# Sparse and forgetting attention on one core: row spreads of inverse roots and forget biases by DMA, index products in four groups

## The chip, the core and the metric

The kernel runs on one core of a Trainium2 chip. The metric is the device time of one execution in microseconds (us); less is better. It computes in float32 throughout. Large matrix products are made from three passes: an operand is rounded to a short form ("hi", type fp32r) with the rest kept as a second one ("lo"), and hi*hi, hi*lo and lo*hi are summed in PSUM.

## What is computed

A trunk of two layers on 512 positions of width 1024. Each layer has a SwiGLU feed-forward half step, a mixer, another half step and a normalisation. The mixer of layer one is DSA, that of layer two FoX. Cut to what matters here:

```python
# DSA: an index score picks 128 keys per query
dots  = relu(einsum('bqhd,bsd->bqhs', iq, ik))        # 8 index heads of 64
score = einsum('bqh,bqhs->bqs', iw, dots)             # masked, then top_k
k = rms_norm(k, k_gain)                               # 2 key heads of 128
# FoX: 8 heads of 128
k = rms_norm(k, k_gain)
cum = cumsum(log_sigmoid(fz + f_bias), axis=1)        # one row per head
logits = q @ k.T * scale + cum_of_query - cum_of_key  # the query's term drops out of softmax
p = softmax(where(causal, logits, -inf))
```

## The kernel before

Activations lie transposed: 128 features on the partitions, 512 positions along a row. Weights come in **units** of 1024 x 128. SP loads a unit (512 KB) into a ring of four, ACT rounds it (`hi`, line 411), DVE or POOL makes the rest (`lo`, lines 751 and 345), and PE runs 24 matmuls of 512 columns with it (lines 1297, 1298, 1302; `section` and `unit`). There is no planner: each engine's program is written out by hand and the order of its lines is the order of the work. Semaphores tie the engines together.

**DSA, index part.** Four units give the eight index heads, two heads per unit: an even head on partitions 0 to 63, an odd one on 64 to 127. A product (`score`, lines 1493 to 1495) is three matmuls over 64 rows and 256, 384 or 512 columns, for one head and one of three query blocks (the first block needs none). `dots(g)` makes six, waiting for the copies in PSUM that ACT has still to take. ACT applies relu (line 574), DVE sums with the weights `iw` (lines 1086, 1089). The order is head by head: three blocks of one head, then three of the next. PE runs `dots(0)`, `dots(1)`, unit 4, `dots(2)`, `dots(3)`, then units 5 to 7. Then DVE runs `top_k` for three blocks: 16 rounds each of a maximum and a replacement, with the k work between them. PE meanwhile makes the eight q units.

**Normalising k.** k has positions along the row, so its inverse root has to lie along the row too, the same on all 128 partitions. PE sums the squares with a column of ones (lines 1574 and 1762), DVE turns that to a variance (`var`, lines 1134 and 1260), and POOL raises it to -1/2 (`job`, line 315). The root is then one number per partition and block. DVE splits it in hi and lo (`split_roots`, lines 778 and 779) and PE spreads it with eight matmuls against the identity (`spread`, line 1361). DVE multiplies k by the bank (lines 1141 and 1268), ACT rounds k, and DVE or POOL makes its lo part.

**FoX, head j.** PE runs unit q, unit k, the bias (`fox_bias`, lines 1741 and 1742), ten transposes of the head before (`fox_turn`, line 1708), half of unit v, the values of the head before (`fox_pv`, line 1720), the sums of squares (line 1762), the other half of v, half of the gate unit, the spread, four transposes of v (line 1772), the rest of the gate unit, and the scores (`fox_score`, lines 1493 to 1495 and 1731). The bias is row j of `cum` on all partitions: two matmuls over eight rows of `cum_hi` and `cum_lo`, copied by ACT to `fox_nb` (`keep_nb`, line 684) and added by DVE at line 1278. `forget_sums` (lines 1206 to 1211) makes `cum` once, in head 0, before the k multiplication of line 1268.

```python
                pe.wait_ge(root_ready, 8 + j)
                spread(bank[FOX_RB[1]], 9 + j, NB).then_inc(k_rb, 1)
                pe.wait_ge(evicted, n + 3)
```

Of the kernel before, what the change touches and what calls it, by code (L numbers as in the profile page):

```python
# [90 lines left out]
def build(nc, xt, cvec, columns, mod_t, w_units, out):  # L91
    ctx = ExitStack()
    with ctx:
# [92 lines left out]
        cum_hi, cum_lo = hid_hi[0:HEADS, KT - 1, :], hid_lo[0:HEADS, KT - 1, :]  # L186
# [7 lines left out]
        K_BANK, V_BANK = (2, 6), (6, 1)  # L194
# [37 lines left out]
        qk_sq, qk_stat, k_rb, k_ready = sem("qk_sq"), sem("qk_stat"), sem("k_rb"), sem("k_ready")  # L232
# [161 lines left out]
        ROOTS_BEFORE = [0, 1, 3, 4, 5, 6, 15, 16]  # L394
# [8 lines left out]
        def _(act):  # L403
# [278 lines left out]
            def keep_nb(j):  # L682
                act.wait_ge(nb_done, j + 1)
                act.activation(fox_nb[:, j % 2, :], bank[OB], ACT.Copy).then_inc(nb_ready, 1)

            for j in range(HEADS):
# [35 lines left out]
                if j == 0:  # L722
                    keep_nb(0)
# [13 lines left out]
        def _(dve):  # L737
# [341 lines left out]
            def index_sums(g):  # L1079
                for m in range(6 * g, 6 * g + 6):  # L1080
                    b, head = m % 3 + 1, m // 3
# [3 lines left out]
                    if head == 0:  # L1085
# [148 lines left out]
            for j in range(HEADS):  # L1234
# [21 lines left out]
                lo(n + 5)  # L1256
# [611 lines left out]
```

## Time and profile before

| | |
|---|---|
| median of 3 runs | 2023.62 us (2021.04 to 2023.71) |
| the profiled execution | 2023.55 us, its span 2021.7 us |
| busy PE / PE weight load | 98% / 81% |
| busy DVE / ACT / POOL | 55% / 36% / 10% |
| granted TensorE clock, mean | 0.993 |
| DMA | 253.97 MB, mean 126 GB/s |

The span is what the profile covers; the 1.85 us between it and the execution's own time lie around it. An end of a matmul is modelled: a 512-column matmul reads 0.39 us, but the next begins 0.23 us after it. So times on PE are read as distances between starts.

### The profile page before, as it was taken

What the parts mean: (1) busy time and instruction counts of PE and PEld (TensorE: products, weight loads), DVE (VectorE), ACT (ScalarE), POOL (GpSimd) and SP (SyncE); (2) the same over time, 40 slices, a digit from 0 to 9 for tenths busy, and PEclk for the clock granted to TensorE, in tenths of its full rate; (3) what the DMA queues carried; (4) which work ended last, traced back from release to release, by engine and by line L of the source; (5) the groups of instructions that cost most, each with busy time, mean ns of one, the idle gap of its engine ahead of it and who ended that gap; (6) DMA issues with size and microseconds to landing.
All of it is one profiled execution on the core that took longest, in us unless ns stands there. A gap on an engine that the chain in (4) does not pass through costs nothing.

```text
span 2021.7 us, 23587 instructions
## 1 busy us (share of the span) xinstructions
PE 1986.2 (98%) x9174; PEld 1645.4 (81%) x9174; DVE 1109.7 (55%) x1705; ACT 726.7 (36%) x1066; POOL 193.4 (10%) x221
## 2 busy tenths in 40 slices
PE   6999999999999999999999999999999999999997
PEld 4888888888888888888888888877888888888886
DVE  7665553788757655636863553475454573333334
ACT  5222312554644222225322222345555442222223
POOL 3110000026600100000110100000000000000000
PEclk9999999999999999999999999999999999999998
DMA  8665542322025655623553632222221122323221
GB/s 318 239 214 180 184 156 88 100 87 74 22 98 194 216 172 194 189 77 108 188 190 104 205 125 83 94 84 64 73 72 54 63 94 104 104 83 108 81 87 57
DMA packets 72014, 253.97 MB, mean 126 GB/s; under 512 B 8025, under 2 KB 8153, under 8 KB 71938
## 3 DMA queue, kind: packets, MB, share of 16 engines
q1 hardware_dynamic: 53280, 185.62, 28.0%
q0 software_dynamic: 18512, 67.26, 10.0%
q8 instruction: 46, 0.75, 0.1%
q14 instruction: 30, 0.25, 0.0%
q10 hardware_dynamic: 146, 0.09, 0.0%
HBM read 250.70 MB, written 2.10 MB: 125 GB/s over the span
## 4 chain that ended last, share of the span: by engine, by line
PE 76%; issue 19%; DVE 3%; POOL 1%; ACT 1%; DMA 0%; POOLq 0%; SPq 0%; DVEq 0%; ACTq 0%
PE bank L1297 23%; PE bank L1302 23%; PE bank L1298 23%; PE bank L1762 1%; PE bank L1720 1%; PE bank L1361 1%; PE bank L1651 1%; PE bank L1493 1%; PE bank L1495 1%; DVE dve_tmp L876 1%; PE bank L1494 0%; PE bank L1708 0%; DVE wlo L751 0%; PE bank L1626 0%; DVE h_lo L869 0%
## 5 line engine op out<-in xcount | busy, mean ns | idle before, releaser
L1297 PE MATMUL bank<-h_hi,whi 128*128 128x512 f32 x1808 | 712.3, 394 | 6.8 <-DVE wlo L751 4.5
L1298 PE MATMUL bank<-h_hi,wlo 128*128 128x512 f32 x1808 | 706.1, 391 | 0.0
L1302 PE MATMUL bank<-h_lo,whi 128*128 128x512 f32 x1808 | 594.1, 390 | 0.5 <-POOL h_lo L331 0.5
L411 ACT ACTIVATE whi<-wraw 128x1024 fp32r<-128x1024 f32 x338 | 347.1, 1053 | 267.0 <-PE bank L1302 263.9
L751 DVE TENSOR_TENSOR wlo<-wraw,whi 128x1024 fp32r<-128x1024 f32 x324 | 389.2, 1223 | 57.3 <-ACT whi L411 56.5
L1297 PEld LDWEIGHTS bank<-h_hi,whi 128*128 128x128 f32 x1808 | 341.2, 189 | 79.3 <-issue 5.0
L1302 PEld LDWEIGHTS bank<-h_lo,whi 128*128 128x128 f32 x1808 | 340.5, 188 | 73.1 <-POOL h_lo L331 1.2
L1298 PEld LDWEIGHTS bank<-h_hi,wlo 128*128 128x128 f32 x1808 | 341.0, 189 | 68.6
L1297 PE MATMUL bank<-hid_hi,whi 128*128 128x512 f32 x832 | 324.3, 390 | 0.0
L1302 PE MATMUL bank<-hid_lo,whi 128*128 128x512 f32 x832 | 323.7, 389 | 0.0
L1298 PE MATMUL bank<-hid_hi,wlo 128*128 128x512 f32 x832 | 323.7, 389 | 0.0
L956 DVE TENSOR_TENSOR dve_tmp<-act_tmp,bank 128x512 f32<-128x512 f32 x85 | 58.5, 689 | 458.6 <-ACT act_tmp L478 458.6
L478 ACT ACTIVATE act_tmp<-bank 128x512 f32<-128x512 f32 x85 | 51.0, 600 | 624.3 <-PE bank L1302 624.2
L1302 PEld LDWEIGHTS bank<-hid_lo,whi 128*128 128x128 f32 x832 | 156.2, 188 | 32.6
L1298 PEld LDWEIGHTS bank<-hid_hi,wlo 128*128 128x128 f32 x832 | 156.2, 188 | 32.4
L1297 PEld LDWEIGHTS bank<-hid_hi,whi 128*128 128x128 f32 x832 | 156.2, 188 | 32.0
L904 DVE SCALAR_TENSOR_TENSOR xT<-bank,gate,xT 128x512 f32<-128x512 f32 x96 | 72.1, 751 | 170.0 <-PE bank L1302 169.9
L315 POOL TENSOR_TENSOR rstd<-var,minus_half 128x8 f32<-128x8 f32 (+2 forms) x19 | 33.3, 1753 | 1119.0 <-DVE var L786 759.6
L763 DVE CUSTOM_DVE_ANT_0 arena<-arena,cond,cols 128x1024 f32<-128x1024 f32 x96 | 121.1, 1280 | 0.0
L310 POOL DMA_DIRECT2D arena<-in_mod_t_dram x96 | 50.7, 529 | 309.0 <-DVE modc L763 309.0
L962 DVE TENSOR_TENSOR hid_lo<-dve_tmp,hid_hi 128x512 fp32r<-128x512 f32 x88 | 60.5, 687 | 21.3 <-ACT hid_hi L481 19.2
L428 ACT ACTIVATE sq<-xT 128x512 f32<-128x512 f32 x42 | 26.6, 633 | 72.2 <-DVE xT L904 72.2
(239 smaller groups left out, 1390.1 us busy)
## 6 DMA issues: line engine op xcount, KB each, us to landing
wraw<-in_w_units_dram SPq DMA_DIRECT2D x306, 512.0 KB, 3.5
arena<-in_mod_t_dram POOLq DMA_DIRECT2D x96, 512.0 KB, 4.9
mod_tile<-in_mod_t_dram POOLq DMA_DIRECT2D x32, 512.0 KB, 4.7
wraw<-in_w_units_dram SPq DMA_DIRECT2D x32, 384.0 KB, 3.4
arena<-in_mod_t_dram SPq DMA_DIRECT2D x12, 512.0 KB, 7.9
xT<-in_xt_dram SPq DMA_DIRECT2D x8, 256.0 KB, 4.5
out_dram<-xT SPq DMA_DIRECT2D x8, 256.0 KB, 2.3
mod_tile<-in_mod_t_dram SPq DMA_DIRECT2D x2, 512.0 KB, 9.5
```

What stands on the lines that cost most here:

```text
L310: pool.dma_start(tile_slot(t), mod_t[t, :, :]).then_inc(ring_in[t % MOD_RING], 16)
L315: pool.tensor_tensor(rstd[:, j % 2, at:at + n], var[:, j % 2, at:at + n], minus_half[:, 0:n], ALU.pow)\
L411: act.activation(whi[:, s % RING, :, :], wraw[:, s % RING, :, :], ACT.Copy).then_inc(hi_ready, 1)
L478: act.activation(act_tmp[:, q, :], bank[s % 4][:, :], ACT.Silu).then_inc(act_out, 1)
L751: dve.tensor_tensor(wlo[:, s % RING, :, :], wraw[:, s % RING, :, :], whi[:, s % RING, :, :].bitcast(F32), ALU.subtract).then_inc(lo_ready, 1)
L763: dve.tensor_tensor_reduce(out=src, in0=src, in1=cond_wide if t < MOD_FIRST else cond[:, :], scale=1.0, scalar=cols[:, col:col + 1], op0=A ...
L904: dve.scalar_tensor_tensor(out=xT[:, bass.ds(i * 4 + d, 1), :], in0=bank[at].unsqueeze(1), scalar=g[:, bass.ds(i * 4 + d, 1)], in1=xT[:, b ...
L956: dve.tensor_tensor(dve_tmp[:, q, :], act_tmp[:, q, :], bank[(s + 1) % 4][:, :], ALU.mult)\
L962: dve.tensor_tensor(hid_lo[:, n, :], dve_tmp[:, q, :], hid_hi[:, n, :].bitcast(F32), ALU.subtract).then_inc(hid_ready, 1)
L1297: pe.matmul(dst, whi[:, w, k, :], hi_, start=first, stop=False)
L1298: pe.matmul(dst, wlo[:, w, k, :], hi_, start=False, stop=False)
L1302: return pe.matmul(dst, whi[:, s % RING, k, :], lo_, start=False, stop=last)
```

## The change

1. **k roots by DMA.** POOL writes the root to a row in device memory (`k_roots`), waits, and reads it back on all 128 partitions: in DSA once for both key heads, in FoX once per head. `split_roots` and `spread` go for k. DVE multiplies by the copy in SBUF, reading it with a step of four elements (`from_row`).
2. **Forget biases by DMA.** `cum` is written to device memory once; `fetch_bias(j)` reads row j on all partitions into `fox_nb`. `fox_bias`, `keep_nb` and the split of `cum` go.
3. **FoX order.** For j > 0 the sums of squares come right after `fox_turn`, in bank 5, and DVE takes `var` before the next `lo` and the output of the head before.
4. **Index products.** `dot_at` makes even and odd heads take turns, product by product. The four groups lie one after `dots(0)`, in the middle and at the end of unit 4, and in the middle of unit 5.

```diff
+def dot_at(m):
+    return m % 3 + 1, 2 * (m // 6) + m % 2
...
+        fox_kb, dsa_kb = sq[:, 1, :], pt_lo[:, 0:KV_HEADS * SEQ].bitcast(F32)
...
@@ POOL, DSA
             job(2, 8)
+            pool.wait_ge(rstd_ready, 3)
+            pool.dma_start(k_roots[HEADS:HEADS + KV_HEADS, :].rearrange("g (p b) -> p g b", b=NB),
+                           rstd[:, 0, 0:KV_HEADS * NB].rearrange("p (g b) -> p g b", g=KV_HEADS)).then_inc(root_out, 16)
+            pool.wait_ge(root_out, 16)
+            pool.dma_start(dsa_kb.rearrange("p (g n) -> p g n", g=KV_HEADS),
+                           k_roots[HEADS:HEADS + KV_HEADS, :].unsqueeze(0).broadcast_to([P, KV_HEADS, SEQ]))\
+                .then_inc(root_in, 16)
...
@@ POOL, FoX
+            def fetch_bias(j):
+                if j > 1:
+                    pool.wait_ge(masked, NB * (HEADS + j - 1))
+                pool.dma_start(fox_nb[:, j % 2, :], cum_rows[j:j + 1, :].broadcast_to([P, SEQ])).then_inc(nb_in[j % 2], 16)
+
             for j in range(HEADS):
                 job(9 + j, 8)
+                pool.wait_ge(rstd_ready, 10 + j)
+                pool.dma_start(k_roots[j, :].rearrange("(p b) -> p b", b=NB), rstd[:, (9 + j) % 2, NB:2 * NB])\
+                    .then_inc(root_out, 16)
+                pool.wait_ge(root_out, 16 * (j + 2))
+                if j:
+                    pool.wait_ge(qk_normed, 2 + j)
+                pool.dma_start(fox_kb, k_roots[j:j + 1, :].broadcast_to([P, SEQ])).then_inc(root_in, 16)
+                if j == 0:
+                    pool.wait_ge(cum_ready, 1)
+                    pool.dma_start(cum_rows[:, :], cum[0:HEADS, :]).then_inc(cum_out, 16)
+                    pool.wait_ge(cum_out, 16)
+                    fetch_bias(0)
+                if j + 1 < HEADS:
+                    fetch_bias(j + 1)
...
@@ ACT, FoX
                 if j:
-                    keep_nb(j)
                     fox_rounds(j - 1)
...
@@ DVE, DSA
             top_k(1, 13, 16)
-            split_roots(2, 2 * NB)
             top_k(2, 0, 4)
+            dve.wait_ge(root_in, 16)
             for g in range(KV_HEADS):
-                dve.wait_ge(k_rb, g + 1)
-                dve.tensor_tensor(dsa_k[:, g, :], dsa_k[:, g, :], bank[K_BANK[g]][:, :], ALU.mult)\
+                dve.tensor_tensor(by_block(dsa_k[:, g, :]), by_block(dsa_k[:, g, :]),
+                                  from_row(dsa_kb[:, g * SEQ:(g + 1) * SEQ]), ALU.mult)\
                     .then_inc(qk_normed, 1)
...
@@ DVE, forget_sums and FoX
-                link(dve.tensor_tensor_scan(cum[0:HEADS, :], sq[0:HEADS, 0, :], z, 0.0, ALU.mult, ALU.subtract))
-                link(dve.tensor_copy(cum_hi, cum[0:HEADS, :]))
-                dve.tensor_tensor(cum_lo, cum[0:HEADS, :], cum_hi.bitcast(F32), ALU.subtract).then_inc(cum_ready, 1)
+                dve.tensor_tensor_scan(cum[0:HEADS, :], sq[0:HEADS, 0, :], z, 0.0, ALU.mult, ALU.subtract)\
+                    .then_inc(cum_ready, 1)
...
                     fox_splits(j - 1)
-                lo(n + 5)
+                else:
+                    lo(n + 5)
+                dve.wait_ge(qk_stat, 10 + j)
+                dve.tensor_scalar(var[:, (9 + j) % 2, 0:8], bank[FOX_STAT][:, 0:8], 1.0, HD * EPS, ALU.mult, ALU.add)\
+                    .then_inc(var_ready, 1)
                 if j:
+                    lo(n + 5)
                     fox_output(j - 1)
-                dve.wait_ge(qk_stat, 10 + j)
-                dve.tensor_scalar(var[:, (9 + j) % 2, 0:8], bank[STAT][:, 0:8], 1.0, HD * EPS, ALU.mult, ALU.add)\
-                    .then_inc(var_ready, 1)
-                split_roots(9 + j, 2 * NB)
                 lo(n + 6)
                 if j == 0:
                     forget_sums()
-                dve.wait_ge(k_rb, 3 + j)
+                dve.wait_ge(root_in, 16 * (j + 2))
                 dve.wait_ge(evicted, n + 2)
-                dve.tensor_tensor(fox_qk[:, 1, :], fox_qk[:, 1, :], bank[FOX_RB[1]], ALU.mult).then_inc(qk_normed, 1)
+                dve.tensor_tensor(by_block(fox_qk[:, 1, :]), by_block(fox_qk[:, 1, :]), from_row(fox_kb), ALU.mult)\
+                    .then_inc(qk_normed, 1)
                 dve.wait_ge(qk_rounded, 4 + 2 * j)
                 dve.tensor_tensor(qk[:, 3, :], fox_qk[:, 1, :], qk[:, 1, :].bitcast(F32), ALU.subtract)\
                     .then_inc(k_ready, 1)
                 split_v(j % 2, bank[FOX_VB], 3 + j)
-                dve.wait_ge(nb_ready, j + 1)
...
@@ PE, DSA
                 for m in range(6 * g, 6 * g + 6):
-                    b, head = m % 3 + 1, m // 3
+                    b, head = dot_at(m)
...
             dots(0)
-            dots(1)
-            plain(4)
-            dots(2)
-            dots(3)
-            for n in range(5, 8):
+            for n in range(4, 6):
+                begin(U + n, U + n - 1)
+                for part in range(2):
+                    section(U + n, bank[(U + n) % 2], 4 * part, 4 * part + 4, h_hi, h_lo)
+                    if n == 4 or part == 0:
+                        dots(2 * n - 7 + part)
+            for n in range(6, 8):
                 plain(n)
...
                 if j:
                     dsa_q_stat(j - 1)
-                if j == 0:
-                    pe.wait_ge(root_ready, 3)
-                    for g in range(KV_HEADS):
-                        spread(bank[K_BANK[g]], 2, NB * g).then_inc(k_rb, 1)
...
@@ PE, FoX
-            def fox_bias(j):
-                if j == 0:
-                    pe.wait_ge(cum_ready, 1)
-                else:
-                    pe.wait_ge(nb_ready, j)
-                if j > 1:
-                    pe.wait_ge(gated, j - 1)
-                head = ident_r[0:HEADS, j:j + 1].broadcast_to([HEADS, P])
-                pe.matmul(bank[OB], head, cum_hi, start=True, stop=False)
-                pe.matmul(bank[OB], head, cum_lo, start=False, stop=True).then_inc(nb_done, 1)
+            def fox_stat(j):
+                pe.wait_ge(qk_sq, 12 + 2 * j)
+                for q in range(2):
+                    for b in range(NB):
+                        ins = pe.matmul(bank[FOX_STAT][:, NB * q + b:NB * q + b + 1], act_tmp[:, q, b * P:(b + 1) * P],
+                                        ones[:, 0:1], start=True, stop=True)
+                ins.then_inc(qk_stat, 1)
...
                 if j:
-                    fox_bias(j)
                     fox_turn(j - 1)
+                    fox_stat(j)
                 begin(n + 2, n + 1 if j else U)
                 section(n + 2, bank[n % 2], 0, 4, h_hi, h_lo)
                 if j:
                     fox_pv(j - 1)
-                pe.wait_ge(qk_sq, 12 + 2 * j)
-                for q in range(2):
-                    for b in range(NB):
-                        ins = pe.matmul(bank[STAT][:, NB * q + b:NB * q + b + 1], act_tmp[:, q, b * P:(b + 1) * P],
-                                        ones[:, 0:1], start=True, stop=True)
-                ins.then_inc(qk_stat, 1)
+                else:
+                    fox_stat(j)
                 section(n + 2, bank[n % 2], 4, KT, h_hi, h_lo)
                 begin(n + 3, n + 2)
                 section(n + 3, bank[(n + 1) % 2], 0, 4, h_hi, h_lo)
-                pe.wait_ge(root_ready, 8 + j)
-                spread(bank[FOX_RB[1]], 9 + j, NB).then_inc(k_rb, 1)
                 pe.wait_ge(evicted, n + 3)
                 for b in range(NB):
                     ins = pe.transpose(bank[FOX_VB][:, b * P:(b + 1) * P], fox_vT[:, b * P:(b + 1) * P], ident[:, :])
                 ins.then_inc(v_turned, 1)
                 section(n + 3, bank[(n + 1) % 2], 4, KT, h_hi, h_lo)
-                if j == 0:
-                    fox_bias(0)
                 fox_score(j)
```

**PE, FoX, head 1, from the end of unit k.** Line 1708 (after: 1745) is `fox_turn`, 1762 (after: 1773) the sums of squares. Before:

```order
L1302 MATMUL bank<-h_lo,whi 128x512
L1741 MATMUL bank<-hid_hi,ident_r 128x512 [waits nb_ready]
L1742 MATMUL bank<-hid_lo,ident_r 128x512
L1708 MATMUL bank<-ident,arena 128x128 [waits fox_split,v_ready,p_ready]
L1708 MATMUL bank<-ident,arena 128x128 x9
L1297 MATMUL bank<-h_hi,whi 128x512 [waits evicted,lo_ready]
```

After:

```order
L1341 MATMUL bank<-h_lo,whi 128x512
L1745 MATMUL bank<-ident,arena 128x128 [waits fox_split,v_ready,p_ready]
L1745 MATMUL bank<-ident,arena 128x128 x9
L1773 MATMUL bank<-ones,act_tmp 128x1 [waits qk_sq]
L1773 MATMUL bank<-ones,act_tmp 128x1 x7
L1336 MATMUL bank<-h_hi,whi 128x512 [waits evicted,lo_ready]
```

The two bias matmuls are gone and the sums of squares have come up to here from behind `fox_pv`.

**POOL, FoX, heads 0 and 1.** Before, POOL had one operation per head here. After:

```order
L334 TENSOR_TENSOR rstd<-var,minus_half 128x8 [waits var_ready]
L415 DMA k_roots<-rstd 128x4 [waits rstd_ready]
L420 DMA sq<-k_roots 128x512 [waits root_out]
L423 DMA cum_rows<-arena 8x512 [waits cum_ready]
L410 DMA arena<-cum_rows 128x512 [waits cum_out]
L410 DMA arena<-cum_rows 128x512
L334 TENSOR_TENSOR rstd<-var,minus_half 128x8 [waits var_ready]
L415 DMA k_roots<-rstd 128x4 [waits rstd_ready]
L420 DMA sq<-k_roots 128x512 [waits qk_normed,root_out]
L410 DMA arena<-cum_rows 128x512 [waits masked]
```

Each head now has a chain of two transfers behind its root, and the bias of the next head follows it on the same queue.

**PE, DSA, the end of `dots(0)`.** Before, `dots(1)` follows at once:

```order
L1493 MATMUL bank<-hid_hi 128x512
L1494 MATMUL bank<-hid_lo,hid_hi 128x512
L1495 MATMUL bank<-hid_hi,hid_lo 128x512
L1493 MATMUL bank<-hid_hi 128x256 [waits relu_ready,evicted]
L1494 MATMUL bank<-hid_lo,hid_hi 128x256
```

After, the first half of unit 4 stands between them:

```order
L1532 MATMUL bank<-hid_hi 128x512
L1533 MATMUL bank<-hid_lo,hid_hi 128x512
L1534 MATMUL bank<-hid_hi,hid_lo 128x512
L1336 MATMUL bank<-h_hi,whi 128x512 [waits evicted,lo_ready]
L1337 MATMUL bank<-h_hi,wlo 128x512
```

## Rows read from the trace of the kernel before

**Rows 1.** Waits of PE, whole span: us in total, times, longest.

```profile
PE bank L1762 <- ACT act_tmp L700: 2.8, 1, 2.8
```

**Rows 2.** Timeline of PE, FoX head 2: start us, duration us, instruction.

```profile
1414.81 0.39 PE L1298 MATMUL bank<-h_hi,wlo 128*128 128x512 f32 x1
1415.04 0.39 PE L1302 MATMUL bank<-h_lo,whi 128*128 128x512 f32 x1
...
1416.01 1.31 PE L1708 MATMUL bank<-ident,arena 128*128 128x128 f32 x10
...
1421.77 1.89 PE L1762 MATMUL bank<-ones,act_tmp 128*128 128x1 f32 x16
...
1429.08 1.00 PE L1361 MATMUL bank<-ident_r,root 128*128 128x128 f32 x8
1429.92 0.63 PE L1772 MATMUL bank<-ident,arena 128*128 128x128 f32 x4
...
1433.13 0.22 PE L1493 MATMUL bank<-qk 128*128 128x128 f32 x1
```

**Rows 3.** Timelines of DVE and POOL, FoX head 2.

```profile
1423.97 0.16 DVE L1260 TENSOR_SCALAR var<-bank 128x8 f32<-128x8 f32 x1
...
1424.21 1.64 POOL L315 TENSOR_TENSOR rstd<-var,minus_half 128x8 f32<-128x8 f32 x1 [29.50 <-DVE var L1260]
...
1428.14 1.23 DVE L751 TENSOR_TENSOR wlo<-wraw,whi 128x1024 fp32r<-128x1024 f32 x1 [1.88 <-ACT whi L411]
1430.12 0.69 DVE L1268 TENSOR_TENSOR arena<-arena,bank 128x512 f32<-128x512 f32 x1 [0.76 <-PE bank L1361]
```

**Rows 4.** DMA issues: count, KB each, median us from issue to landing.

```profile
arena<-in_mod_t_dram POOLq DMA_DIRECT2D x96, 512.0 KB, 4.9
...
mod_tile<-in_mod_t_dram SPq DMA_DIRECT2D x2, 512.0 KB, 9.5
...
act_tmp<-arena POOLq DMA_DIRECT2D x1, 16.0 KB, 2.0
```

**Rows 5.** Timelines of DVE and PE, FoX head 0.

```profile
1366.02 0.41 DVE L1210 CAST hid_hi<-arena 8x512 fp32r<-8x512 f32 x1
...
1367.08 0.67 DVE L1268 TENSOR_TENSOR arena<-arena,bank 128x512 f32<-128x512 f32 x1
...
1369.19 0.33 PE L1493 MATMUL bank<-qk 128*128 128x128 f32 x1 [1.13 <-DVE qk L1270]
```

**Rows 6.** Busy us (count) of PE, weight load, DVE, ACT, POOL; clock; DMA.

```profile
1360.00:1395.00 35.00, 33.87 (x169) 27.46 (x169) 18.98 (x37) 17.65 (x31) 1.64 (x1) 0.95 0.20 61
```

**Rows 7.** Timeline of PE, DSA index products and what follows them.

```profile
415.39 0.38 PE L1493 MATMUL bank<-hid_hi 64*128 64x256 f32 x1 [0.58 <-DVE hid_lo L1100]
...
416.43 0.28 PE L1494 MATMUL bank<-hid_lo,hid_hi 64*128 64x256 f32 x1
...
416.60 0.39 PE L1494 MATMUL bank<-hid_lo,hid_hi 64*128 64x512 f32 x1
...
420.44 0.50 PE L1297 MATMUL bank<-h_hi,whi 128*128 128x512 f32 x1
...
426.11 0.38 PE L1493 MATMUL bank<-hid_hi 64*128 64x256 f32 x1
...
430.70 0.50 PE L1297 MATMUL bank<-h_hi,whi 128*128 128x512 f32 x1
```

**Rows 8.** Timeline of PE, DSA, the spread for both key heads.

```profile
454.46 1.90 PE L1361 MATMUL bank<-ident_r,root 128*128 128x128 f32 x16
```

**Rows 9.** Timelines of DVE and POOL during top_k, with their idle time in brackets.

```profile
449.12 0.17 DVE L1134 TENSOR_SCALAR var<-bank 128x8 f32<-128x8 f32 x1 [1.57 <-PE bank L1574]
...
451.36 1.67 POOL L315 TENSOR_TENSOR rstd<-var,minus_half 128x8 f32<-128x8 f32 x1
...
458.60 1.28 DVE L1141 TENSOR_TENSOR arena<-arena,bank 128x512 f32<-128x512 f32 x2
...
494.74 0.18 DVE L1146 TENSOR_SCALAR var<-bank 128x24 f32<-128x24 f32 x1 [4.04 <-PE bank L1586]
```

More of the change, by code:

```diff
@@ L185, in build, with by_block, from_row @@
         cum = piece(4864, SEQ)
-        cum_hi, cum_lo = hid_hi[0:HEADS, KT - 1, :], hid_lo[0:HEADS, KT - 1, :]
+        fox_kb, dsa_kb = sq[:, 1, :], pt_lo[:, 0:KV_HEADS * SEQ].bitcast(F32)
+        def by_block(ap):
+            return ap.rearrange("q (b p) -> q b p", b=NB)
+        def from_row(ap):
+            return ap.rearrange("q (p b) -> q b p", b=NB)
         low = [ctx.enter_context(nc.psum_tensor(f"bank{i}", [P, SEQ], F32)) for i in range(4)]
@@ L231, in build @@
             sem("ik_spread"), sem("iw_turned"), sem("dots_done"), sem("relu_ready"), sem("relu_used"))
-        qk_sq, qk_stat, k_rb, k_ready = sem("qk_sq"), sem("qk_stat"), sem("k_rb"), sem("k_ready")
+        qk_sq, qk_stat, k_ready = sem("qk_sq"), sem("qk_stat"), sem("k_ready")
+        root_out, root_in, cum_out = sem("root_out"), sem("root_in"), sem("cum_out")
+        nb_in = [sem("nb_in0"), sem("nb_in1")]
         v_turned, v_rounded, v_ready = sem("v_turned"), sem("v_rounded"), sem("v_ready")
@@ L240, in build @@
         fz_ready, ls_ready, cum_ready = sem("fz_ready"), sem("ls_ready"), sem("cum_ready")
-        nb_done, nb_ready, scaled = sem("nb_done"), sem("nb_ready"), sem("scaled")
+        scaled = sem("scaled")
         gsq_ready, gsum_added = sem("gsq_ready"), sem("gsum_added")
         stored = sem("stored")
+        k_roots = nc.dram_tensor("k_roots", (HEADS + KV_HEADS, SEQ), F32).ap()
+        cum_rows = nc.dram_tensor("cum_rows", (HEADS, SEQ), F32).ap()
         block = ctx.enter_context(nc.Block())
@@ L393, in build @@
         POST_RB = 4
-        ROOTS_BEFORE = [0, 1, 3, 4, 5, 6, 15, 16]
+        ROOTS_BEFORE = list(range(8))
         LAST_UNIT = {st: down + KT + 3 for st, down in (
@@ L569, in relus @@
                 for m in range(6 * g, 6 * g + 6):
-                    w = (m % 3 + 2) * P
+                    w = (dot_at(m)[0] + 1) * P
                     act.wait_ge(dots_done, m + 1)
@@ L680, in fox_scale @@
                                    scale=rstd[:, (9 + j) % 2, b:b + 1]).then_inc(scaled, 1)
-            def keep_nb(j):
-                act.wait_ge(nb_done, j + 1)
-                act.activation(fox_nb[:, j % 2, :], bank[OB], ACT.Copy).then_inc(nb_ready, 1)
             for j in range(HEADS):
@@ L1084, in index_sums @@
                     dve.wait_ge(relu_ready, m + 1)
-                    if head == 0:
+                    if m < 3:
                         ins = dve.tensor_scalar(sc, relu[:, m % 4, 0:w], iw[:, at:at + 1], None, ALU.mult)
@@ L1272, in _ @@
                 split_v(j % 2, bank[FOX_VB], 3 + j)
-                dve.wait_ge(nb_ready, j + 1)
+                dve.wait_ge(nb_in[j % 2], 16 * (j // 2 + 1))
                 for b in range(NB):
@@ L1544, in dots @@
                 for m in range(6 * g, 6 * g + 6):
-                    b, head = m % 3 + 1, m // 3
+                    b, head = dot_at(m)
                     if m >= 6:
```

7 lines of the change are left out of this document (2 added, 5 removed).

## The prediction, made before the changed kernel was run

> **What bounds the kernel now.** I read the engines' shares first: PE is busy 98% of the span, the next engine, DVE, 55%. Then the list of who PE waited for. In the two stages that the change touches it holds only small items, the largest 2.8 us, once, in FoX head 0 [rows 1]. So PE's own work sets the pace, and a matmul taken out of it is time gained, as long as nothing else becomes late. The timeline of PE in a FoX head shows the pace: two 512-column matmuls start 0.23 us apart, while each reads 0.39 [rows 2]. I therefore price everything on PE by distances between starts. The question of the change is then whether two transfers through device memory fit under the work that stands between a root and its use.
>
> **FoX, the bias, per head.** Unit k's last matmul starts at 1415.04 and would hand over at 1415.27. The transposes start at 1416.01 [rows 2]. The two bias matmuls and their changeover thus cost 0.74 us. The spread costs 1429.92 - 1429.08 = 0.84 us [rows 2]. Together 1.58 us per head. Moving the sums of squares changes no amount of work on PE.
>
> **FoX, does the root come in time?** In before's own times, for head 2: the transposes now start at 1415.27 and take at most 1.3, the sums of squares 1.9 [rows 2], so `var` is made at about 1418.8, with the 0.3 that lie between sums and `var` today. POOL's power starts 0.24 later and takes 1.64 [rows 3]: the root is there at 1420.7. The step that needs it follows the `lo` of line 751 on DVE. That one waits for ACT and so for PE; it moves up with the bias, from 1428.14 to 1427.4, and ends at 1428.6 [rows 3]. So two transfers have 7.9 us before DVE waits at all. From the k multiplication to the first score head 0 takes 1369.19 - 1367.08 = 2.1 us [rows 5]; the scores are due at 1433.13 - 1.58 = 1431.55 [rows 2], so PE waits only if the row lands after 1429.4, which is 8.7 us behind the root.
>
> What a round trip costs no row shows. The first transfer writes 2 KB; the nearest row is 16 KB on POOL's queue, 2.0 us to landing. The second writes 256 KB into SBUF, between the 16 KB with 2.0 and the 512 KB on POOL's queue with 4.9 [rows 4]. So 4.0 to 6.9 us. I take 6, nearer the 512 KB, because the weights share the engines (0.20 of their time in this stage [rows 6]). It is hidden, with 1.9 us to DVE's step and 2.7 to PE's. The multiplication reads SBUF with a step of four elements instead of a bank; no row has that. I take today's 0.69 [rows 3], and even twice that would use 0.7 of the 2.7.
>
> The Trainium skill, DMA: Bandwidth & Descriptors ("Anatomy of one DMA"), gives about 2.0 us plus bytes over 436 GB/s for one DMA from POOL's queue; as an estimate from that page the round trip would be 2.0 + 2.6 = 4.6 us, and the sum would stay the same.
>
> **FoX, head 0.** Here the k multiplication stands behind `forget_sums` on DVE, and PE already waits 1.13 us for it. Leaving out the split of `cum` brings it from 1367.08 to about 1366.0 [rows 5], so the scores come 1.1 us earlier and no more; the other 0.5 of the 1.58 turns into waiting. The root has time: its sums are in the old place, and `forget_sums` covers it. The first bias row needs two more transfers after `cum`, some 4 to 7 us; it may hold DVE up by about 1 us, with ten and more us before PE needs that head's probabilities. FoX in all: 7 x 1.58 + 1.1 = **12.2 us**. ACT loses eight copies and DVE sixteen short steps; neither bounds, so nothing for that.
>
> **DSA, the spread.** Sixteen matmuls read 1.90 us with the last one's tail of about 0.2 [rows 8]; twice 0.84 says the same: **1.7 us**.
>
> **DSA, the index products.** Today they take 420.44 - 415.39 = 5.05 and 430.70 - 426.11 = 4.59, together 9.64 us [rows 7]. The columns are 24 x 3 x 384 = 27,648; at 0.23 us per 512 that is 12.4 us one after another, so today some products already run beside others. One sees where: at 416.43 a 256-column matmul of head 1's first product starts, and at 416.60 a 512-column one of head 0's last, which stands ahead of it in the program [rows 7]. The two halves of the rows run side by side there, each at its own pace. Today that happens only where one head follows another. Taking turns, it can happen everywhere: 6.2 us as the floor. Four groups have four changeovers and four ragged ends instead of two; with 0.3 us for each (the bias's changeover above is of that size) 7.4. Gain **2.2 us**; bounds are -0.5 (four groups at today's rate, plus two changeovers) and 3.4 (the floor). ACT and DVE now get six products per half unit and more; DVE's sums took 0.55 us each before, 3.3 per group against 1.85 + 2.75 on PE, so PE does not wait for copies.
>
> **DSA, is DVE late then?** The gain counts only if top_k keeps up. DVE waits for PE today: 1.57 us before `var` and 4.04 before the variances of the q heads [rows 9]. With PE 2.2 us earlier, `var` comes at 446.9, the root at 453.03 - 2.2 = 450.8 (POOL is busy with a `lo` before), the row after two transfers of 4.0 to 6.9 (512 KB, so the far end) at 454.8 to 457.7. DVE wants it at 446.9 + 9.5 (from 449.12 to 458.60 [rows 9]) less 1.0 for the split and its wait: 455.4. It waits 0 to 2.3 us. It then reaches the q variances at 490.70 - 2.2 - 1.0 = 487.5 plus that wait, 489.8 at worst; PE delivers at 494.74 - 3.9 = 490.8. Hidden, by 1 us or more. POOL is held for the first transfer, 2 us or so, in a stretch where it idles. DSA: **3.9 us**.
>
> **Sum.** 12.2 + 1.7 + 2.2 = 16.1 us. The profiled execution took 2023.55 us (span 2021.7 and 1.85 around it), 0.07 below the median, so the two are the same here. 2023.55 - 16.1 = **2007.4 us**.
>
> **The rivals.** *A: the products don't overlap more* (2009.6). If matmuls start strictly in program order, one product overlaps the next only by its last matmul, and a group of six keeps about today's 2.4 us. Against it stand the two starts out of order [rows 7]; the Trainium skill, TensorE: Matmul & The Clock Gate (Part 2, step 1), speaks for it: matmuls stay in program order, only weight loads are pulled ahead. By that rule the sum would be 13.9; the trace does not agree with it.
>
> *B: DVE bounds DSA* (2011.3). If root row or index sums come later than I think, top_k ends where it does today and the 3.9 us are spent waiting. The reserve is 1 us at the far end.
>
> *C: the root comes late in FoX* (slower). From 8.7 us for the round trip PE waits in every head, ahead of its scores. After the 1.13 us wait of head 0 the clock of the next 35 us averages 0.95 [rows 6], which is 1.75 us more. The whole 16.1 us is given back by a wait of 0.3 us per head (if the clock falls each time) to 2.0 us (if it never does); slower begins at a round trip of 9.0 to 10.7. With 12, a wait of 3.3 and 1.75 of clock: 8 x (3.3 + 1.75) - 16 = 24 us, 2048 us. For it: the 2 KB leave in 128 pieces of 16 bytes, and a transfer landed only after 9.5 us [rows 4]. Against: that one stood in the crowd at the program's start. The Trainium skill, DMA page again (Specifications, and its rules for authors), says that pieces under 512 bytes miss the line rate and are read, changed and written, one descriptor each: it speaks for C, without a price.
>
> *D: small waits* (2009 to 2013): the root 0.5 us late per head, or head 0's longer wait (1.6 us for 1.13) with one more stretch at half clock, 1.75 us. The opposite, that stretch avoided, would be 2005.7.
>
> **Chances.** Forecast 0.60 (2004 to 2009), A 0.14, B 0.10, D 0.11, C 0.04, and 0.01 that a spread is still waited for elsewhere and nothing moves. The floor for the products and head 0's clock taken off give 2004.5, fewer changeovers on PE perhaps 1 us more; B with a part of D reaches 2013 to 2014. The range is 2003.5 to 2014. A change of 0.2%, 4 us, is about what can be told from none. Faster by more: 0.94; within: 0.03; slower: 0.03.
>
> **What would show it.** A FoX head in the new profile should go from one k unit to the next in 1.6 us less, with no wait of PE ahead of the scores and none of DVE for the root row. The two transfers should take 4 to 7 us. The first and last product of a group should be 1.6 us apart. DVE should still wait before the q variances. A wait of PE for the k part in each head, or a mean clock below 0.99, would make the prediction wrong.

## The result, and the profile after

The changed kernel takes 2011.17 us (median of 6 runs, 2010.29 to 2012.00) against 2023.25 (6 runs, 2020.42 to 2023.71): ratio 0.9944, 95% interval 0.9931 to 0.9957. It is faster by 12.1 us; predicted were 16.1. So 2011.2 lies in the range of 2003.5 to 2014, but above the 2004 to 2009 that the forecast had for itself. The profiled execution took 2011.08 us with a span of 2009.0, so its span is 12.7 us shorter. The table below takes distances on PE between starts of the same instructions in both traces.

| stretch on PE | before | after | difference | predicted |
|---|---|---|---|---|
| first index product to the scores of DSA head 0 | 85.88 | 82.14 | -3.7 | -3.9 |
| first index product to the scores of DSA head 2 | 96.70 | 96.88 | +0.2 | -3.9 |
| sums of squares of FoX head 0 to `shift_columns` behind FoX | 297.2 | 284.8 | -12.4 | -12.2 |

DSA saves its 3.7 us on PE and gives all of it back within two heads. FoX gives what was asked of it.

**The index products** went as forecast. PE of the changed kernel, first and last record of the first and the fourth group, and what follows each:

```profile
415.13 0.45 PE L1532 MATMUL bank<-hid_hi 64*128 64x256 f32 x2 [0.58 <-DVE hid_lo L1138]
...
416.63 0.39 PE L1534 MATMUL bank<-hid_hi,hid_lo 64*128 64x512 f32 x2
416.95 0.50 PE L1336 MATMUL bank<-h_hi,whi 128*128 128x512 f32 x1
...
429.43 0.45 PE L1532 MATMUL bank<-hid_hi 64*128 64x256 f32 x2
...
431.25 0.50 PE L1336 MATMUL bank<-h_hi,whi 128*128 128x512 f32 x1
```

A group takes 416.95 - 415.13 = 1.82 us, and the fourth 431.25 - 429.43 = 1.82 too: 7.3 us for four, where [rows 7] give 9.64. Starts are again out of the program's order: the fourth product's first matmul starts at 415.77, the third product's second, which stands ahead of it in the program, at 415.83.

**DVE in DSA** did not keep up. DVE of the changed kernel, from `var` of k to the row maxima:

```profile
447.23 0.17 DVE L1172 TENSOR_SCALAR var<-bank 128x8 f32<-128x8 f32 x1
450.25 0.29 DVE L1168 TENSOR_SCALAR arena<-arena 128x256 f32<-128x256 f32 x1
...
457.58 2.41 DVE L1178 TENSOR_TENSOR arena<-arena,pt_lo 128x512 f32<-128x512 f32 x2 [1.85 <-DMA pt_lo<-k_roots]
...
474.92 1.58 DVE L1168 TENSOR_SCALAR arena<-arena 128x384 f32<-128x384 f32 x1
...
491.90 0.18 DVE L1184 TENSOR_SCALAR var<-bank 128x24 f32<-128x24 f32 x1
...
501.10 2.41 DVE L1168 TENSOR_SCALAR arena<-arena 128x512 f32<-128x512 f32 x1
...
505.67 0.17 DVE L1046 TENSOR_SCALAR negmax<-rowmax 128x4 f32<-128x4 f32 x1
```

`var` comes without a wait, 1.9 us earlier than in [rows 9]. Then DVE waits 1.85 us for the root row, and the two multiplications take 2.41 us instead of 1.28. It reaches the variances of the q heads at 491.90 with no wait left, where it had 4.04 us in [rows 9]. Line 1168 is the last step of `top_k`, which turns the scores into a mask: 1.58 us for 384 elements and 2.41 for 512, against 0.53 and 1.19 before. POOL in the same stretches:

```profile
449.17 1.66 POOL L334 TENSOR_TENSOR rstd<-var,minus_half 128x8 f32<-128x8 f32 x1
...
453.48 0.57 POOL L374 DMA_DIRECT2D pt_lo<-k_roots  x1 [1.54 <-DMA k_roots<-rstd]
...
455.67 2.37 POOL L364 TENSOR_TENSOR wlo<-wraw,whi 128x1024 fp32r<-128x1024 f32 x1
...
473.88 2.40 POOL L364 TENSOR_TENSOR wlo<-wraw,whi 128x1024 fp32r<-128x1024 f32 x1
...
500.83 2.39 POOL L364 TENSOR_TENSOR wlo<-wraw,whi 128x1024 fp32r<-128x1024 f32 x1
```

POOL's operations end at 476.28 and 503.22, and DVE's two long steps 0.22 and 0.29 us behind them. The same steps before the change, and POOL beside the second:

```profile
474.82 0.53 DVE L1130 TENSOR_SCALAR arena<-arena 128x384 f32<-128x384 f32 x1
...
503.94 1.19 DVE L1130 TENSOR_SCALAR arena<-arena 128x512 f32<-128x512 f32 x1
```

```profile
503.56 1.28 POOL L360 TENSOR_TENSOR hid_lo<-act_tmp,hid_hi 128x512 fp32r<-128x512 f32 x1
```

POOL's operation ends at 504.84 and DVE's step 0.29 us later, so the step was held before the change too, by a shorter operation.

PE pays for the lateness in front of the scores of head 1, whose last product is shown too:

```profile
497.27 0.31 PE L1532 MATMUL bank<-qk,hid_hi 128*128 128x128 f32 x1
...
505.69 0.39 PE L1532 MATMUL bank<-qk,hid_hi 128*128 128x128 f32 x1 [2.61 <-DVE rowmax L1039]
...
508.01 0.63 PE L1532 MATMUL bank<-qk,hid_hi 128*128 128x512 f32 x1
508.43 0.63 PE L1533 MATMUL bank<-qk,hid_hi 128*128 128x512 f32 x1
```

After the wait of 2.61 us the 512-column matmuls start 0.42 us apart instead of 0.23: PE runs at the lower of its two levels, 1.2 GHz. The granted clock of the stretch, behind the busy times, says the same (0.97):

```profile
501.00:550.00 49.00, 44.37 (x270) 39.26 (x269) 37.89 (x115) 31.57 (x94) 32.22 (x30) 0.97 0.07 22
```

From the scores of head 1 to the scores of head 2 are 512.01 - 505.69 = 6.3 us, against 4.8 before, so 1.5 more.

**FoX.** A head, from its transposes to those of the next, takes 1442.13 - 1412.63 = 29.5 us; the same distance was 31.1 before. Head 2 on DVE, POOL and PE:

```profile
1415.65 0.16 DVE L1296 TENSOR_SCALAR var<-bank 128x8 f32<-128x8 f32 x1
1415.73 1.22 DVE L789 TENSOR_TENSOR wlo<-wraw,whi 128x1024 fp32r<-128x1024 f32 x1
...
1425.87 1.07 DVE L1306 TENSOR_TENSOR arena<-arena,sq 128x512 f32<-128x512 f32 x1
1427.64 0.69 DVE L1309 TENSOR_TENSOR qk<-arena,qk 128x512 fp32r<-128x512 f32 x1 [0.70 <-ACT qk L757]
```

```profile
1415.90 2.57 POOL L334 TENSOR_TENSOR rstd<-var,minus_half 128x8 f32<-128x8 f32 x1 [23.49 <-DVE var L1296]
1418.76 0.61 POOL L415 DMA_DIRECT2D k_roots<-rstd  x1 [0.29 <-POOL rstd L334]
1420.85 0.54 POOL L420 DMA_DIRECT2D sq<-k_roots  x1 [1.48 <-DMA k_roots<-rstd]
```

```profile
1428.86 0.22 PE L1532 MATMUL bank<-qk 128*128 128x128 f32 x1
```

The row left at 1420.85 and landed 4.1 us later, at 1424.92, which is 6.5 us behind the end of the power (1418.47) and 0.95 before DVE takes it. (In heads 1 to 7 it landed 6.0 to 6.8 us behind the power and 0.65 to 1.4 us before DVE took it.) The multiplication takes 1.07 us, not 0.69. DVE's last step for k ends at 1428.33, 0.5 before the scores, and PE does not wait. The waits of PE:

```profile
PE bank L1532 <- DVE rowmax L1039: 2.6, 1, 2.6
PE bank L1532 <- DVE qk L1309: 1.8, 1, 1.8
```

The second is the wait for the k part: once in eight heads, ahead of the scores of head 0 at 1368.18. It was 1.13 in [rows 5]. The transfers, count, KB and median time to landing, which [rows 4] had only from others:

```profile
sq<-k_roots POOLq DMA_DIRECT2D x8, 256.0 KB, 3.7
arena<-cum_rows POOLq DMA_DIRECT2D x8, 256.0 KB, 3.8
pt_lo<-k_roots POOLq DMA_DIRECT2D x1, 512.0 KB, 4.0
k_roots<-rstd POOLq DMA_DIRECT2D x8, 2.0 KB, 1.9
```

### The profile page after: what moved, and what is told of

Same layout as the page of the kernel before. It is cut to its first block, busy times and chain, and to the rows that moved or that the text cites. A ratio compares the mean times of both kernels' runs of the same rounds, so it can differ in the third digit from the quotient of the medians.

```text
span 2009.0 us, 23394 instructions
## 1 busy us (share of the span) xinstructions
PE 1967.9 (98%) x9078; PEld 1630.6 (81%) x9078; DVE 1109.9 (55%) x1685; ACT 719.4 (36%) x1058; POOL 215.3 (11%) x248
## 4 chain that ended last, share of the span: by engine, by line
PE 73%; issue 19%; DVE 5%; POOL 1%; ACT 1%; DMA 0%; POOLq 0%; SPq 0%; DVEq 0%; ACTq 0%
PE bank L1336 23%; PE bank L1341 22%; PE bank L1337 22%; DVE arena L1166 1%; DVE top L1165 1%; PE bank L1773 1%; PE bank L1756 1%; PE bank L1532 1%; PE bank L1688 1%; PE bank L1534 1%; PE bank L1533 1%; DVE dve_tmp L914 1%; PE bank L1745 0%; PE bank L1663 0%; DVE h_lo L907 0%
## 5 line engine op out<-in xcount | busy, mean ns | idle before, releaser
L334 POOL TENSOR_TENSOR rstd<-var,minus_half 128x8 f32<-128x8 f32 (+2 forms) x19 | 39.9, 2099 | 1063.9 <-DVE var L824 759.1
```

What stands on the lines that cost most here:

```text
L334: pool.tensor_tensor(rstd[:, j % 2, at:at + n], var[:, j % 2, at:at + n], minus_half[:, 0:n], ALU.pow)\
```

## The experiments

The theory, T: the forecast's gain of 3.9 us in DSA was made on PE and lost on DVE, by the wait for the row, by operations that POOL holds up, and by the lower clock after PE's wait. Its first rival: DSA kept its gain and FoX gave less.

Every run is compared with runs of the kernel before on the same chip. The stretch behind FoX, from `shift_columns` to the end of the span, took 366.4 to 374.1 us in these traces, and no edit lies there (in the changed kernel 371.6). So I also give **D**, the distance on PE from the first index product to `shift_columns` behind FoX, and **d**, that to the scores of DSA head 2. Both come from the one profiled execution of each kernel. The kernel before took 2021.57 to 2023.25 us beside them, so a total belongs next to the one in its own row; the intervals are about 2.6 us wide, and differences of 2 to 4 us between changed kernels rest on d and D.

| kernel | us | before beside it | ratio, 95% interval | d | D |
|---|---|---|---|---|---|
| before | | | 1 | 96.70 | 1234.5 |
| changed | 2011.17 | 2023.25 | 0.9944, 0.9931 to 0.9957 | 96.88 | 1222.3 |
| fox_only | 2011.52 | 2021.57 | 0.9946, 0.9932 to 0.9960 | 96.71 | 1222.3 |
| dsa_root_undone | 2007.66 | 2021.57 | 0.9933, 0.9920 to 0.9947 | 94.77 | 1218.7 |
| dots_only | 2019.57 | 2021.57 | 0.9987, 0.9978 to 0.9996 | 94.78 | 1231.9 |
| mult_late | 2007.41 | 2021.57 | 0.9932, 0.9918 to 0.9945 | 92.98 | 1216.9 |
| mask_stepped | 2011.51 | 2022.94 | 0.9944, 0.9931 to 0.9958 | 96.90 | 1222.3 |
| forget_early | 2009.90 | 2022.94 | 0.9935, 0.9922 to 0.9949 | 96.89 | 1218.7 |
| three_moves | 2004.47 | 2022.94 | 0.9911, 0.9896 to 0.9926 | 92.97 | 1214.8 |
| fox_write_twice | 2021.55 | 2022.94 | 1.0001, 0.9991 to 1.0012 | 98.32 | 1236.8 |
| mask_accum | 2006.97 | 2022.45 | 0.9925, 0.9912 to 0.9939 | 92.60 | 1216.5 |
| three_moves_no_turns | 2008.55 | 2022.45 | 0.9932, 0.9918 to 0.9945 | 96.09 | 1218.2 |
| row_in_order | 2084.31 | 2022.45 | 1.0306, 1.0292 to 1.0320 | 96.78 | 1299.5 |

### fox_only

```diff
-    return m % 3 + 1, 2 * (m // 6) + m % 2
+    return m % 3 + 1, m // 3
...
+            split_roots(2, 2 * NB)
             top_k(2, 0, 4)
-            dve.wait_ge(root_in, 16)
```

and on PE the old places of `dots` and the two spreads.

> Changed kernel with its DSA parts undone (index products in the old order and places, root of k split by DVE and spread by PE); FoX stays changed. Theory T (the DSA gain of 3.9 us was all lost again to a late DVE: row wait 1.85, slower operations, half clock after a 2.61 us wait of PE): as fast as the changed kernel, 2011.2 us within 0.7. Rival (DSA gained 3.9 as forecast and FoX gave only 8 us of its 12.2): 2015.1 us.

Measured: 2011.52 us, and D to 0.1 us that of the changed kernel, 1222.3. FoX alone makes the whole gain of the change, and the DSA parts together are worth nothing. The first rival falls.

### dsa_root_undone

The root of k in DSA as in the diff above; the products stay changed.

> Changed kernel, only the DSA root of k goes back to split and spread; products in four groups and FoX stay. T: PE has 1.7 us more to do, but DVE has no row to wait for and reads a bank (0.64 instead of 1.2 us each), so PE's scores of head 1 are due at 504.8 and are not waited for; no half clock. 2011.2 - 0.9 - 1.5 = 2008.8 us, faster than the changed kernel although PE does more. Rival (the spread's removal is worth its 1.7 us on PE): 2012.9 us.

Measured: 2007.66 us. d falls by 2.1 us against the changed kernel, though PE reaches the scores of head 0 1.8 us later (83.96 for 82.14). PE waits 0.22 us ahead of head 1, and the clock of 501 to 550 us is 1.00, where the changed kernel has 0.97. D falls by 3.6 us; the other 1.5 lie between the sums of squares and the scores of FoX head 0, which nothing edited here touches: after the same wait of 2.8 us for the squares the clock of 1340 to 1360 us is 0.91 here and 0.83 in the changed kernel. As put in there, this part of the change costs more than it brings. DVE in this kernel has its reserve again:

```profile
456.64 1.29 DVE L1172 TENSOR_TENSOR arena<-arena,bank 128x512 f32<-128x512 f32 x2
472.86 0.53 DVE L1161 TENSOR_SCALAR arena<-arena 128x384 f32<-128x384 f32 x1
492.78 0.18 DVE L1177 TENSOR_SCALAR var<-bank 128x24 f32<-128x24 f32 x1 [4.03 <-PE bank L1620]
```

### dots_only

The kernel before with `dot_at` and the new places of `dots`, as in the diff of the change.

> Kernel before, only the index products changed (turns, four groups). T: 2.2 us less on PE and DVE has its 4 us of reserve before the q variances, with no row to wait for: 2023.5 - 2.2 = 2021.3 us. Rival (DVE or ACT eats it, the products' gain never counts): 2023.5 us.

Measured: 2.0 us less, the interval 0.8 to 4.4; d falls by 1.9. So the products' gain counts as long as DVE is in time. I had put it at 2.2. The four groups are 2.4 us shorter than the two were (7.3 for 9.64), so 0.4 to 0.5 us of that is lost again around them, in the changeovers.

### mult_late

```diff
-            top_k(2, 0, 4)
+            top_k(2, 0, 6)
             dve.wait_ge(root_in, 16)
...
-            top_k(2, 4, 16)
+            top_k(2, 6, 16)
```

> Changed kernel; in DSA DVE takes the k multiplication two rounds of top_k later (after round 6 of block 2 instead of 4). T: the 1.85 us wait for the root row goes, and the multiplication starts at the same time as now (457.6). DVE ends its masks 1.85 us sooner, PE's wait for the row maxima falls from 2.61 to about 0.8: 2009.3 us, 2007.8 if the clock no longer falls. Rival (DVE is not what PE waits for, or the wait moves elsewhere): 2011.2 us.

Measured: 2007.41 us, and d shorter by 3.9 us: the whole of the lost gain is back, as in the lower of the two times expected. By the totals it is 14.2 us under the kernel before beside it, where the changed kernel was 12.1. DVE of this kernel:

```profile
459.00 2.10 DVE L1178 TENSOR_TENSOR arena<-arena,pt_lo 128x512 f32<-128x512 f32 x2
473.53 1.32 DVE L1168 TENSOR_SCALAR arena<-arena 128x384 f32<-128x384 f32 x1
491.45 0.18 DVE L1184 TENSOR_SCALAR var<-bank 128x24 f32<-128x24 f32 x1 [1.24 <-PE bank L1627]
...
500.95 0.92 DVE L1168 TENSOR_SCALAR arena<-arena 128x512 f32<-128x512 f32 x1
```

The wait for the row is gone, and the last mask step fell on another, shorter operation of POOL and took 0.92 us instead of 2.41. PE waits 0.26 us. D shrinks by 5.4 us, 1.5 more than d: the clock of 1360 to 1395 us is 1.00 here, not 0.95, after nearly the same wait of about 1.8 us in FoX head 0. I changed nothing there, and why the clock held is open.

### mask_stepped and mask_accum

```diff
-                    link(dve.tensor_scalar(sc, sc, (TAKEN + OUTSIDE) / 2, MASKED, ALU.is_gt, ALU.mult))
+                    step = sc.rearrange("p (n t) -> p t n", t=2)
+                    link(dve.tensor_scalar(step, step, (TAKEN + OUTSIDE) / 2, MASKED, ALU.is_gt, ALU.mult))
```

> Changed kernel; the last step of top_k (compare and multiply in one operation on SBUF) goes through its rows with a step of two elements, the same elements and result. In the changed kernel it took 1.58 us for 384 elements and 2.41 for 512, each ending just after an operation of POOL. T (POOL's operation holds this kind of DVE operation up, not the others beside it; stepped it is not of that kind): 0.54 and 0.68 us, as the replacements of the same width take; DVE 2.7 us sooner, PE's wait of 2.61 all but gone, no half clock: 11.2 - 2.6 - 1.5, so 4 us under the changed kernel, 16 under before: 2007.1 us where before is 2023.3. Rival (the operation is long in itself): it stays at 1.2 us or more, and the time at 2011.2.

Measured: 2011.51 us, d and D as in the changed kernel; the two steps took 1.59 and 2.42 us. My expectation failed: a step of two elements changes nothing. It did not speak for the rival either, since the steps again ended 0.2 to 0.3 us behind POOL's. The Trainium skill, VectorE: DVE Perf Modes ("What auto-detection actually checks"), gives a reason: an operation with one source and its result in SBUF goes over both ports when their outermost dimensions are even, and no condition is set on the step; mine became two. So I took a form with an accumulator output:

```diff
-                    link(dve.tensor_scalar(sc, sc, (TAKEN + OUTSIDE) / 2, MASKED, ALU.is_gt, ALU.mult))
+                    link(dve.tensor_scalar(sc, sc, (TAKEN + OUTSIDE) / 2, MASKED, ALU.is_gt, ALU.mult,
+                                           accum_out=step_sum[:, 0:1]))
```

> Changed kernel; the last step of top_k gets an accumulator output beside its own (a sum per row that nobody reads; with it the operation's result may differ, the later work does not depend on values). A step of two elements left the operation as it was (1.59 and 2.42 us, ending with POOL's). T: it is held because it reads and writes by two SBUF port pairs, which this form does not, at half the rate: 0.5 to 0.7 us whatever POOL does, DVE 2.7 us sooner, PE's wait of 2.61 gone, no half clock: 4 us under the changed kernel, 2007.1 where before is 2023.3. Rival (POOL holds any such operation on SBUF, or these are long in themselves): again 1.6 and 2.4 us and 2011.2.

DVE and POOL of mask_accum:

```profile
450.81 0.42 DVE L1169 TENSOR_SCALAR_CACHE_REDUCE arena<-arena 128x256 f32<-128x256 f32 x1
...
475.49 0.55 DVE L1169 TENSOR_SCALAR_CACHE_REDUCE arena<-arena 128x384 f32<-128x384 f32 x1
...
500.64 0.69 DVE L1169 TENSOR_SCALAR_CACHE_REDUCE arena<-arena 128x512 f32<-128x512 f32 x1
```

```profile
474.44 2.40 POOL L365 TENSOR_TENSOR wlo<-wraw,whi 128x1024 fp32r<-128x1024 f32 x1
...
500.15 1.27 POOL L387 TENSOR_TENSOR hid_lo<-act_tmp,hid_hi 128x512 fp32r<-128x512 f32 x1
```

This kernel does not compute the reference's result: with the accumulator the mask comes out otherwise. It serves for the times alone. Not held, the old form takes 0.29 us for 256 elements and this one 0.42. For 384 the new one takes 0.55, in the middle of the same operation of POOL that made it 1.58 in the changed kernel; for 512 it takes 0.69, where the old one took 2.41. The time is 2006.97 us and d 4.3 shorter, where T said 4; D is shorter by 5.8, the other 1.5 again by the clock of 1360 to 1395 us. Shown by this: POOL holds up the fast form and not the slow one. That it is by the ports, as the expectation has it, these rows do not show. Both of DVE's operations ran wholly inside a row of POOL (474.44 to 476.84, 500.15 to 501.42).

### forget_early

```diff
-                lo(n + 6)
                 if j == 0:
                     forget_sums()
+                lo(n + 6)
                 dve.wait_ge(root_in, 16 * (j + 2))
```

> Changed kernel; in FoX head 0 DVE makes forget_sums before the lo step of the gate unit instead of after it, in 5.75 us in which it idles. T (PE's wait of 1.81 us ahead of head 0's scores stands on DVE's order alone): the k multiplication comes 2.4 us sooner, the wait goes; 1.8 us under the changed kernel (2009.4 where before is 2023.3), 3.5 if the clock then stays up (2007.6). Rival (another releaser comes just behind, ACT or the v part): no change, 2011.2.

Measured: 2009.90 us. PE's wait ahead of head 0's scores is gone, the scores come 1.86 us sooner, and D is 3.5 us shorter, the far end of what was expected: the clock of 1360 to 1395 us is 0.99. The total shows 1.0 to 1.3 us of it. In the profiled execution the stretch behind FoX took 374.1 us, against 371.6 in the changed kernel, and the clock from 1850 us to the end was 0.94 for 0.96. DVE of this kernel:

```profile
1358.32 1.21 DVE L1247 TENSOR_TENSOR_SCAN arena<-sq,dve_tmp 8x512 f32<-8x512 f32 x1
...
1363.34 1.09 DVE L1306 TENSOR_TENSOR arena<-arena,sq 128x512 f32<-128x512 f32 x1
```

### three_moves, and without taking turns

> mult_late, mask_stepped and forget_early together on the changed kernel. T: the first two remove the same wait, so 4.0 us once, and 1.8 to 3.5 of head 0: 2003.7 to 2005.4 us where before is 2023.3 (18 to 19.6 less). Rival (the waits move on to the next place): 2007 or more.

Measured: 2004.47 us, 0.9911, D shorter by 7.5 than the changed kernel's. This is the fastest kernel of the study with the reference's computation left whole; mask_stepped is in it and does nothing. On it, the old order of the products in the new places, by the edit of `dot_at` shown under fox_only:

> three_moves with the index products in the old order, head by head, in the four places as they are. T (taking turns is what shortens them): a group takes 2.4 us instead of 1.82, 2.3 us slower than three_moves (2004.5), so 2006.8 where before is 2022.9. Rival (the four places do it, or DVE hides it): 2004.5.

Measured: 2008.55 us; D is longer by 3.4 and d by 3.1. PE, the first group:

```profile
415.68 0.38 PE L1533 MATMUL bank<-hid_hi 64*128 64x256 f32 x1 [0.58 <-DVE hid_lo L1138]
...
418.26 0.50 PE L1337 MATMUL bank<-h_hi,whi 128*128 128x512 f32 x1
```

That is 2.58 us for a group, 0.76 more than in turns. Four such groups are 10.3 us, more than the 9.64 before the change: the four places alone cost 0.7 us, and taking turns brings 3.0. In this kernel the mask step of 384 elements began 0.08 us before an operation of POOL, and the roles are reversed:

```profile
476.19 0.36 DVE L1169 TENSOR_SCALAR arena<-arena 128x384 f32<-128x384 f32 x1
```

```profile
476.27 1.44 POOL L386 TENSOR_TENSOR hid_lo<-act_tmp,hid_hi 128x512 fp32r<-128x512 f32 x1 [0.24 <-ACT hid_hi L667]
```

DVE takes 0.36 us, the shortest of all these runs for 384 elements, and POOL 1.44 for an operation that takes about 1.3 elsewhere.

### fox_write_twice

```diff
-                pool.wait_ge(root_out, 16 * (j + 2))
+                pool.wait_ge(root_out, 16 * (2 * j + 2))
+                pool.dma_start(k_roots[j, :].rearrange("(p b) -> p b", b=NB), rstd[:, (9 + j) % 2, NB:2 * NB])\
+                    .then_inc(root_out, 16)
+                pool.wait_ge(root_out, 16 * (2 * j + 3))
```

> Changed kernel; in FoX POOL writes the root of every head twice and waits each time, so each row lands 2.35 us later. In head 2 of the changed kernel the row lands 0.9 us before DVE wants it, and the lo of k ends 0.5 us before the scores. T: DVE waits 1.4 us per head, PE 0.9 us: 7 x 0.9 = 6.5 us slower than the changed kernel (2017.7 where before is 2023.3), up to 1.75 us more per head if the clock falls each time (2030). Rival (the reserve is as large as predicted, 2.7 us on PE): 2011.2.

Measured: 2021.55 us, 10.4 us over the changed kernel; D 14.5 longer. The sign and the place are T's, the size is larger:

```profile
PE bank L1535 <- DVE qk L1312: 11.6, 8, 3.4
```

Eight waits, 1.45 us in the mean and not 0.9. The first six are 0.6 to 1.6 us. The last two are 2.5 and 3.4. In the one head a write took 3.7 us to land; in the other the second write left 4.8 us after the first, where it left 2.1 to 2.3 after it in the first seven heads. So a few transfers come far later than the median says. The waits are 9.8 us more than in the changed kernel. The rest of the 14.5 is mostly clock: 0.93 in 1550 to 1600 us, and 1.4 us in DSA, where nothing was edited (d is 98.32 for 96.88, with 0.93 in 501 to 550 us for 0.97). The change thus stood about one write of 2 KB per head from giving back what it had won.

### row_in_order

```diff
-                pool.dma_start(k_roots[j, :].rearrange("(p b) -> p b", b=NB), rstd[:, (9 + j) % 2, NB:2 * NB])\
+                pool.dma_start(k_roots[j, :].rearrange("(b p) -> p b", b=NB), rstd[:, (9 + j) % 2, NB:2 * NB],
...
-                dve.tensor_tensor(by_block(fox_qk[:, 1, :]), by_block(fox_qk[:, 1, :]), from_row(fox_kb), ALU.mult)\
+                dve.tensor_tensor(fox_qk[:, 1, :], fox_qk[:, 1, :], fox_kb, ALU.mult)\
```

> Changed kernel; in FoX the row of roots is written in the order of positions (512 pieces of 4 bytes instead of 128 of 16), and DVE reads it without a step. T: the step of four elements is what makes the k multiplication 1.07 us; it goes to 0.69. The transfer out lands later than its 1.8 us; as long as it is under 2.7 nothing waits (2011.2 where before is 2023.3), with 4 times as long (7.2) PE would wait 4 us per head and the time be 2040 or more. Rival (two inputs in SBUF make the 1.07): it stays at 1.07.

Measured: 2084.31 us. The multiplication takes 0.69 us in all eight heads, so the step of four elements made the 1.07. The transfer of the same 2 KB went from 1.9 to 11.1 us, and PE waits in every head:

```profile
k_roots<-rstd POOLq DMA_DIRECT2D x6, 2.0 KB, 11.1
```

```profile
PE bank L1532 <- DVE qk L1309: 60.5, 8, 9.1
```

The waits are 58.7 us more than in the changed kernel and D is 77.3 longer; the clock is lower as well, 0.979 in the mean for 0.994. The pieces became more and smaller in one edit, and which of the two makes the 11.1 us is not shown.

## Why the prediction was right and where it was wrong

**FoX: right.** 12.2 us were summed, 12.4 came. The bias and the spread gave 1.6 us per head. Head 0 gave 0.9 to its scores for the 1.1 forecast; its wait grew by 0.7 where 0.5 was said. The bias row held DVE up for 3.1 us there, not 1, at no cost to PE, as said.

**FoX, the reserve: too large.** The round trip was taken as 6 us and took 6.5 in head 2, inside 4.0 to 6.9. The reserve on DVE, though, was 0.95 us and not 1.9. On PE it was 1.5 and not 2.7: these 0.95, and the 0.5 by which the last step of k came before the scores. Besides the 0.5 us of the round trip, two terms were mis-sized. POOL's power took 2.57 us beside DVE's `lo`, for 1.64 in [rows 3]; the change itself had put that `lo` right behind `var`. And the multiplication took 1.07 for 0.69. Rival C was nearer than its chance of 0.04 suggests. In one head of mult_late the row landed only 0.25 us before DVE took it, and fox_write_twice and row_in_order are that rival, at +10 and +73 us over the changed kernel. The Trainium skill, DMA: Bandwidth & Descriptors (Specifications, and its rules for authors), warned of pieces under 512 bytes. With 128 pieces of 16 bytes the trace shows no price: 1.9 us, against 1.8 for the 16 KB of `cum` in the same profile. With 512 pieces of 4 bytes row_in_order shows 9.2 us more.

**Index products: right.** 7.3 us against 7.4 forecast, though only 1.9 us of the difference reach d in dots_only, for 2.2 forecast. Rival A falls. three_moves_no_turns shows that the turns bring it, and that four places alone would have cost 0.7 us, about what the lower bound of -0.5 had.

**The spread in DSA: right on PE** (1.8 us for 1.7), and it did not count.

**DSA, is DVE late: this step failed.** "Hidden, by 1 us or more" was wrong, and rival B came true, at the very time given for it (2011.3), with a chance of only 0.10. The range held because it had been drawn around rival B as well; the forecast's own sum had 3.9 us for DSA, and DSA gave nothing. I had the wait for the row (1.85 us, inside 0 to 2.3). The q variances, forecast for 489.8 at worst, were taken at 491.90: `var` came 0.3 later than reckoned, the multiplications took 1.1 more and the first mask step 1.05 more. Some 0.8 of the 1.1 are the step of four elements (1.07 us instead of 0.69, twice); the other 0.3 fell in the first of the two, beside a `lo` of POOL that ended at 458.04. And my account stopped at the variances: behind them lie six rounds and the second mask step, 1.2 us longer. The two mask steps, 2.3 us longer together, fell on operations of POOL. From those PE's wait of 2.61 us, and from that 1.5 us of clock. I had priced an instruction that the change does not touch at what it took before; its time depends on what POOL does at that moment, and the change moved DVE against POOL. Even the 0.53 and 1.19 us of before were held times: in three_moves_no_turns 384 elements took 0.36.

## What to carry to other kernels

Taking work off the engine that bounds moves all the others against each other: follow the next engine to the point where its result is used, not to its last known wait, and price its operations with their company. A row fetched through memory wants its consumer placed later than looks needed; here two rounds of other work, at no cost, were worth 3.9 us. Part of that was that the last mask step then met a shorter operation of POOL, which nobody had planned. A copy through device memory was cheap here in 128 pieces and dear in 512: the order of the row cost more than its bytes.

## What the runs showed of the hardware

- A compare-and-multiply of DVE from SBUF to SBUF took 0.29 us for 256 elements when nothing held it, and 2.41 for 512 when POOL had begun a `lo` 0.27 us before. Wherever it began inside a `lo` or a k step of POOL, it ended 0.2 to 0.3 us after POOL's, in every trace. With an accumulator output it took 0.69 and was not held. The Trainium skill, SBUF — State Buffer ("Who interferes with whom"), states this as a lock that goes to whichever starts first. The `lo` rows agree, and so does the reversed case of three_moves_no_turns. POOL's power does not: the step of 256 elements at 450.25 began inside it (1.66 us from 449.17) and took its 0.29 us all the same.
- The other way round POOL's power beside DVE's `lo` of two SBUF inputs took 2.57 us, against 1.64 without. It ended 1.5 us after DVE's.
- Matmuls over 64 rows from the two row halves, issued in turns, took 1.82 us per six products, head by head 2.58.
- After waits of PE of 1.8 us at the same place the granted clock of the next 35 us was 0.95 in one kernel and 1.00 in another, an effect of 1.5 us that no edit here explains.
